# Weight sums of a Strassen-type product: four VectorE additions replaced by accumulating GpSimd transfers

## What is computed

```python
def swiglu(h, w_gate, w_up, w_down):
    return (jax.nn.silu(h @ w_gate) * (h @ w_up)) @ w_down

x = x + 0.5 * swiglu(rmsnorm(x, norm_ffn1), w1_gate, w1_up, w1_down)
...
x = x + 0.5 * swiglu(rmsnorm(x, norm_ffn2), w2_gate, w2_up, w2_down)
return rmsnorm(x, norm_final)
```

## Time and profile before

| | |
|---|---|
| runs | 2141.56, 1722.46, 1720.77 us; median 1722.46 |
| the profiled execution | 1721.32 us, of which 1719.5 us span |
| TensorE busy | 1706.5 us, 99% of the span |
| VectorE / ScalarE / GpSimd busy | 1226.1 / 845.6 / 204.8 us |
| granted TensorE clock | 0.999 over the span |
| moved | 346.28 MB, mean 201 GB/s |

### The profile page before, as it was taken

The page is one execution under the profiler, slowest core; times in us unless marked ns, Lnnn a source line. Parts: engine busy times, 40 slices in busy tenths (PEclk is TensorE's granted clock), DMA queues, the critical chain, the costliest instruction groups (busy, mean ns, idle before and its releaser), DMA issues.

```text
span 1719.5 us, 20848 instructions
## 1 busy us (share of the span) xinstructions
PE 1706.5 (99%) x7638; PEld 1414.8 (82%) x7638; DVE 1226.1 (71%) x1417; ACT 845.6 (49%) x989; POOL 204.8 (12%) x376
## 2 busy tenths in 40 slices
PE   9999999999999999999999999999999999999998
PEld 7788888888888888888888888888887888888886
DVE  7988888886555566587877888888888865554554
ACT  6555555554444444454554555555555554443443
POOL 0111111111110000000040001111111111100000
PEclk9999999999999999999999999999999999999999
DMA  8666666666665555665544565666666666655552
GB/s 293 190 215 216 213 214 217 213 209 209 207 208 196 196 195 191 209 202 192 170 153 164 196 196 179 216 214 214 213 217 197 216 220 203 232 190 193 193 195 98
DMA packets 186226, 346.28 MB, mean 201 GB/s; under 512 B 11768, under 2 KB 23984, under 8 KB 186032
## 3 DMA queue, kind: packets, MB, share of 16 engines
q1 hardware_dynamic: 172960, 332.51, 58.7%
q0 software_dynamic: 11264, 11.56, 2.4%
q10 hardware_dynamic: 1936, 1.32, 0.3%
HBM read 331.71 MB, written 2.10 MB: 194 GB/s over the span
## 4 chain that ended last, share of the span: by engine, by line
PE 96%; DVE 1%; issue 1%; ACT 1%; DMA 1%; POOL 0%; ACTq 0%; SPq 0%; DVEq 0%
PE banks L508 28%; PE banks L509 27%; PE banks L510 27%; PE banks L611 3%; PE banks L612 3%; PE banks L610 3%; PE banks L494 2%; PE banks L527 1%; PE banks L497 1%; POOL turned L1805 0%; DMA turned<-squared 0%; PE banks L704 0%; DVE w_lo L1412 0%; PE banks L728 0%; DVE w_lo L1181 0%
## 5 line engine op out<-in xcount | busy, mean ns | idle before, releaser
L1181 DVE TENSOR_TENSOR w_lo<-raw,w_hi 128x1024 fp32r<-128x1024 f32 x366 | 449.7, 1232 | 349.9 <-ACT w_hi L852 348.4
L852 ACT ACTIVATE w_hi<-raw 128x1024 fp32r<-128x1024 f32 x366 | 386.6, 1060 | 513.4 <-PE banks L510 487.6
L508 PE MATMUL banks<-w_hi,act 128*128 128x512 f32 x1280 | 499.1, 390 | 3.2 <-DVE w_lo L1412 3.2
L510 PE MATMUL banks<-w_lo,act 128*128 128x512 f32 x1280 | 498.0, 389 | 0.0
L509 PE MATMUL banks<-w_hi,act 128*128 128x512 f32 x1280 | 498.0, 389 | 0.0
L1412 DVE TENSOR_TENSOR w_lo<-raw,w_hi 128x1024 fp32r<-128x1024 f32 (+1 forms) x288 | 328.7, 1159 | 111.4 <-ACT w_hi L991 109.0
L991 ACT ACTIVATE w_hi<-raw 128x1024 fp32r<-128x1024 f32 (+1 forms) x288 | 286.9, 1010 | 223.7 <-PE banks L510 200.5
L508 PE MATMUL banks<-w_hi,h 128*128 128x512 f32 x832 | 323.8, 389 | 0.0
L510 PE MATMUL banks<-w_lo,h 128*128 128x512 f32 x832 | 323.7, 389 | 0.0
L509 PE MATMUL banks<-w_hi,h 128*128 128x512 f32 x832 | 323.7, 389 | 0.0
L508 PEld LDWEIGHTS banks<-w_hi,act 128*128 128x128 f32 x1280 | 240.3, 188 | 54.5 <-DVE w_lo L1412 4.4
(11 more groups left out here) (173 smaller groups left out, 1194.3 us busy)
## 6 DMA issues: line engine op xcount, KB each, us to landing
raw<-in_w_down SPq DMA_DIRECT2D x88, 1024.0 KB, 5.0
raw<-in_w_gate SPq DMA_DIRECT2D x84, 1024.0 KB, 5.3
raw<-in_w_up SPq DMA_DIRECT2D x84, 1024.0 KB, 5.5
raw<-in_w_in SPq DMA_DIRECT2D x32, 1024.0 KB, 5.2
raw<-in_w_out SPq DMA_DIRECT2D x16, 1024.0 KB, 5.0
turned<-squared POOLq DMA_DIRECT2D x320, 32.0 KB, 5.6
raw<-in_w_up SPq DMA_DIRECT2D x8, 512.0 KB, 9.2
raw<-in_w_gate SPq DMA_DIRECT2D x7, 512.0 KB, 9.5
```

The lines of the kernel that those rows point to most:

```text
L508: pe.matmul(dst, operand[:, k, hi], w_hi[:, s, w], start=k == first, stop=False)
L510: mm = pe.matmul(dst, operand[:, k, hi], w_lo[:, s, w], start=False, stop=k == last)
L852: act_e.activation(w_hi[:, s, :], raw[:, (p // 2) % RAW_SLOTS, off:off + PIECE], ACT.Copy).then_inc(hi_ready, 1)
L1181: dve.tensor_tensor(w_lo[:, s, :], raw[:, (p // 2) % RAW_SLOTS, off:off + PIECE], w_hi[:, s, :].bitcast(F32), ALU.subtract).then_inc(lo_re ...
```

## The change

The four sums leave VectorE. GpSimd begins four transfers per superblock that add into their destination (`accum_op=ALU.add`), each with a semaphore of its own, and the buffer `sums` goes:

- T3: low half of up chunk 0 += its high half (SBUF to SBUF), when the chunk has landed
- T1: low half of gate chunk 0 += the low half of up chunk 0, *read again from DRAM*, when piece 1 is split
- T2: the same place += the high half of up chunk 0 (SBUF to SBUF), when T1 (piece 7) is split
- T4: the same place += the high half of gate chunk 0 (SBUF to SBUF), when T2 (piece 11) is split, and behind the 16 transfers of `exchange` on GpSimd

The pieces change places: T3 is piece 5, T1 piece 7, B22 9, T2 11, T4 15. Since gate chunk 0's slot is now in use up to T4, chunks 6 and 7 change slots, chunk 7 may start only when 16 pieces are split, and with it everything that SP has behind it; chunk 2 may start only when the superblock before is wholly split. `square_h` goes from behind piece 11 to behind piece 6, `fold_gate` from behind 17 to behind 19.

```diff
-B11_0, B11_1, B21, T1, T3, B22, T2, T4 = 0, 1, 3, 5, 7, 9, 11, 13
+B11_0, B11_1, B21, T3, T1, B22, T2, T4 = 0, 1, 3, 5, 7, 9, 11, 15
-UP_AT = {14 + n: 4 + 2 * n for n in range(6)}
-SUMS = (T1, T3, T2, T4)
+UP_AT = {13: 4, 14: 6, 16: 8, 17: 10, 18: 12, 19: 14}
+SUMS = (T3, T1, T2, T4)
-FAST_SLOTS = (0, 1, 2, 3, 2, 3, 0, 1)
...
+FAST_SLOTS = (0, 1, 2, 3, 2, 3, 1, 0)
...
-FAST_FREE = (-6, -4, -2, 0, 5, 9, 12, 12)
+FAST_FREE = (-6, -4, 0, 0, 5, 9, 12, 16)
-FOLD_AT = (15, 16, 17)
-MERGE_AT, PRODUCT_AT, SQUARE_H_AT, SPLIT_FAST_AT = 2, 4, 11, 18
+FOLD_AT = (14, 16, 19)
+MERGE_AT, PRODUCT_AT, SQUARE_H_AT, SPLIT_FAST_AT = 2, 4, 6, 18
@@ SP, load_gate_up
+                    if i == FAST_SBS + 1 and c == 2:
+                        sp.wait_ge(lo_ready, first)
@@ ScalarE, round_fast
                 if p in SUMS:
-                    act_e.wait_ge(summed, 4 * nth + SUMS.index(p) + 1)
...
+                    act_e.wait_ge(summed[SUMS.index(p)], 16 * (nth + 1))
@@ VectorE: add_sum goes, with its four calls in fast_gate_up
-                    if p == B11_1:
-                        add_sum(nth, T1, turn, shift)
-                        add_sum(nth, T3, turn, shift)
-                    if p == B22:
-                        add_sum(nth, T2, turn, shift)
-                    if p == T2 - 1:
-                        add_sum(nth, T4, turn, shift)
@@ GpSimd
+            def add_weights(p, slot, src):
+
+                pool.dma_start(raw[:, slot, 0:PIECE].rearrange("p (t n) -> p t n", n=QCOLS), src,
+                               accum_op=ALU.add).then_inc(summed[SUMS.index(p)], 16)
+            def fast_sums(f, i):
+
+                first, shift = fast_first(f, i), 0 if i % 2 else 2
+                gate, up = FAST_SLOTS[0] + shift, FAST_SLOTS[1] + shift
+                pool.wait_ge(raw_landed[up], (f["turn"] + 2 * i + 1) * 16)
+                add_weights(T3, up, second_half(up))
+                pool.wait_ge(lo_ready, first + B11_1 + 1)
+                add_weights(T1, gate, f["up"][0:2 * P, i * QCOLS:(i + 1) * QCOLS]
+                            .rearrange("(t p) n -> p t n", p=P))
+                pool.wait_ge(lo_ready, first + T1 + 1)
+                add_weights(T2, gate, second_half(up))
+                exchange(f["sb"] + i - 1, turned)
+                pool.wait_ge(lo_ready, first + T2 + 1)
+                add_weights(T4, gate, second_half(gate))
```

More of the change, by code:

```diff
@@ L75 @@
 MID_FIRST = GATE_PIECES + ROW_PIECES
-B11_0, B11_1, B21, T1, T3, B22, T2, T4 = 0, 1, 3, 5, 7, 9, 11, 13
+B11_0, B11_1, B21, T3, T1, B22, T2, T4 = 0, 1, 3, 5, 7, 9, 11, 15
 GATE_AT = {2: 4, 4: 6, 6: 8, 8: 10, 10: 12, 12: 14}
-UP_AT = {14 + n: 4 + 2 * n for n in range(6)}
-SUMS = (T1, T3, T2, T4)
+UP_AT = {13: 4, 14: 6, 16: 8, 17: 10, 18: 12, 19: 14}
+SUMS = (T3, T1, T2, T4)
 S5, S7, S2, S12 = range(4)
 P1_BANK, N5_BANK, N7_BANK, R6_BANK = 4, 5, 6, 7
-FAST_SLOTS = (0, 1, 2, 3, 2, 3, 0, 1)
-FAST_CHUNK = {0: (0, 0), 1: (0, 1), 2: (2, 0), 3: (0, 2), 4: (2, 2), 6: (3, 0), 7: (1, 0), 8: (3, 2),
-              9: (1, 2), 10: (4, 0), 11: (1, 2), 12: (4, 2), 14: (5, 0), 15: (5, 2), 16: (6, 0),
-              17: (6, 2), 18: (7, 0), 19: (7, 2)}
-FAST_FREE = (-6, -4, -2, 0, 5, 9, 12, 12)
+FAST_SLOTS = (0, 1, 2, 3, 2, 3, 1, 0)
+FAST_CHUNK = {0: (0, 0), 1: (0, 1), 2: (2, 0), 3: (0, 2), 4: (2, 2), 5: (1, 0), 6: (3, 0), 7: (0, 0),
+              8: (3, 2), 9: (1, 2), 10: (4, 0), 11: (0, 0), 12: (4, 2), 13: (5, 0), 14: (5, 2),
+              15: (0, 0), 16: (6, 0), 17: (6, 2), 18: (7, 0), 19: (7, 2)}
+FAST_FREE = (-6, -4, 0, 0, 5, 9, 12, 16)
 COPY_P1_AT, ROUND_FAST_AT = 8, 17
-FOLD_AT = (15, 16, 17)
-MERGE_AT, PRODUCT_AT, SQUARE_H_AT, SPLIT_FAST_AT = 2, 4, 11, 18
+FOLD_AT = (14, 16, 19)
+MERGE_AT, PRODUCT_AT, SQUARE_H_AT, SPLIT_FAST_AT = 2, 4, 6, 18
 U0, W0 = 48, 64
@@ L189, in layer_kernel @@
         forms = at("forms", [P, 2, 4, 2, P], F32R, fast_at)
-        sums = at("sums", [P, PIECE], F32, fast_at + 8 * PIECE)
         whole = at("whole", [P, 4, 2, P], F32, fast_at + 8 * PIECE)
@@ L258, in layer_kernel @@
         h_squared = sem("h_squared")
-        summed = sem("summed")
+        summed = [sem(f"summed{p}") for p in SUMS]
         whole_act_ready = sem("whole_act_ready")
@@ L980, in round_fast @@
                 act_e.wait_ge(piece_used, first + p - SPLIT_SLOTS + 1)
+                c = FAST_CHUNK[p][0]
+                slot = (FAST_SLOTS[c] + shift) % RAW_SLOTS
                 if p in SUMS:
-                    act_e.wait_ge(summed, 4 * nth + SUMS.index(p) + 1)
-                if p in (T1, T4):
-                    dst, src = w_hi[:, p % SPLIT_SLOTS, :], sums[:, :]
-                else:
-                    c = FAST_CHUNK[p][0]
-                    slot = (FAST_SLOTS[c] + shift) % RAW_SLOTS
+                    act_e.wait_ge(summed[SUMS.index(p)], 16 * (nth + 1))
+                else:
                     act_e.wait_ge(raw_landed[slot], (turn + (1 if c < 4 else 2)) * 16)
-                    off, size = fast_part(p)
-                    dst, src = w_hi[:, p % SPLIT_SLOTS, 0:size], raw[:, slot, off:off + size]
-                act_e.activation(dst, src, ACT.Copy).then_inc(hi_ready, 1)
+                off, size = fast_part(p)
+                act_e.activation(w_hi[:, p % SPLIT_SLOTS, 0:size], raw[:, slot, off:off + size],
+                                 ACT.Copy).then_inc(hi_ready, 1)
             def copy_p1(first, fi):
@@ L1383, in split_forms @@
                 dve.memset(folds[:, :, :], 0.0).then_inc(folded, 1)
[L1385 to L1401, removed]
             def split_fast(first, p, shift):
@@ L1406, in split_fast @@
                 s = p % SPLIT_SLOTS
[L1407 to L1411, removed]
+                off, size = fast_part(p)
+                src = raw[:, (FAST_SLOTS[FAST_CHUNK[p][0]] + shift) % RAW_SLOTS, off:off + size]
                 dve.tensor_tensor(w_lo[:, s, 0:size], src, w_hi[:, s, 0:size].bitcast(F32),
@@ L1457, in fast_gate_up @@
             def fast_gate_up(f, i, shift):
-                turn, first, fi = f["turn"] + 2 * i, fast_first(f, i), f["sb"] + i
+                first, fi = fast_first(f, i), f["sb"] + i
                 nth = f["fast"] + i - 1
@@ L1806, in exchange, with second_half @@
                                      .rearrange("p (t k) j -> p t (k j)", k=SB)).then_inc(h_turned, 16)
+            def add_weights(p, slot, src):
+                pool.dma_start(raw[:, slot, 0:PIECE].rearrange("p (t n) -> p t n", n=QCOLS), src,
+                               accum_op=ALU.add).then_inc(summed[SUMS.index(p)], 16)
+            def second_half(slot):
+                return raw[:, slot, PIECE:2 * PIECE].rearrange("p (t n) -> p t n", n=QCOLS)
+            def fast_sums(f, i):
[11 more added lines that the diff above has]
+                add_weights(T4, gate, second_half(gate))
             for f in ffns:
-                for i in range(1, GATE_SBS):
+                for i in range(1, FAST_SBS + 1):
+                    fast_sums(f, i)
+                for i in range(FAST_SBS + 1, GATE_SBS):
                     exchange(f["sb"] + i - 1, turned)
```

## The result

The changed kernel takes 1805.09 us (1801.42 to 1808.14, four runs), the one before 1721.88 us beside it; the ratio is 1.0485, with an interval of 1.0465 to 1.0506. It is slower by 83 us. One run of before took 2141.56 us; the ratio is of the fast runs alone. The profiled execution took 1801.42 us, of which 1799.4 us are its span.

The account below looks back on a forecast made before the run. TensorE, busy 99% of the span, was taken to bound the kernel, hiding the removed VectorE additions (worth 0). The loop would lengthen superblocks from 42.2 to 47.4 us: 1721.3 + 15 x 5.2 = 1799.3, so 1800 us, range 1730 to 1890.

Parts of the forecast that it names:

- the loop paces: Fast superblocks: the feeding chain from T2 back to T2' sets the pace, X from 6.6 to 12; 1757 to 1920 us, chance 0.60.
- X: Time from issue to landing of one accumulating 512 KB GpSimd transfer: taken as 8.0 us, bounded by 3.3 and 14.1.
- 2X + 31.4: Superblock length in us if T4's issue waits for T2's landing, then round and split of piece 11.
- X + 38.0: Superblock length in us if the exchange on GpSimd, 8.9 us, holds T4's issue in place of T2's landing.
- step 6: After chunk 7 loads: round 18, split 18, split_h, split 19, together 4.6 us.
- T3 and T1 beside the loop: These two transfers lie outside the chain that sets a superblock's length; T1 has 13.9 us to spend.
- It closes 14 times, and half for the last ones: Seven closings per feed-forward part, each part's last superblock counted half: 15 x 5.2 = 78 us lost.
- The clock, for which I set no term: TensorE's clock: stalls of 1 to 4 us spread over 42 should not lower it from 2.4 GHz; no term.
- The signs I named: Exchanges 47 us apart, L1390 waits before pieces 2, 11 or 15 to 18, landing near 8 us, VectorE down 78 us.
- the bound of X = 14.1: Dearest transfer, with GpSimd's issue growing from 0.53 to 4.2 us: superblock 59.6 us, 17.4 us lost.
- Hidden: Rival: transfers land fast, X below 4.2, no TensorE wait at all; 1719 to 1722 us, chance 0.26.
- The DMA engines are the bound: Rival: addition slow inside DMA engines, X 12 and more, queued loads late too; 1900 to 2050 us, chance 0.13.

Follow-up runs that it names:

- experiment 4: Changed kernel with T2 alone made by VectorE, T3, T1 and T4 staying transfers: 1766.67 us, ratio 1.0255.
- experiment 2: Changed kernel with T2 and T4 made by VectorE, only T1 and T3 staying accumulating transfers: 1723.65 us, ratio 1.0007.
- experiment 5: Changed kernel with T1, T3 and T2 made by VectorE, only T4 staying an accumulating transfer: 1766.41 us, ratio 1.0258.
- experiment 1: Changed kernel, its piece order and load table kept, with all four sums made again by VectorE: 1725.88 us, ratio 1.0021.
- experiment 11: Kernel before the change with square_h behind piece 8 instead of 11, nothing else: 1719.50 us, ratio 0.9989.
- experiment 8: Changed kernel with all four transfers as plain copies, the sums left out: 1754.82 us, ratio 1.0199.
- experiment 6: Changed kernel with the exchange behind T4 on GpSimd instead of ahead of it: 1805.44 us, ratio 1.0485.
- experiment 7: Changed kernel with T2 made by VectorE and the exchange behind T4: 1771.62 us, ratio 1.0292.
- experiment 9: Changed kernel with T4's transfer alone a plain copy, its sum left out, the other three accumulating: 1784.20 us, ratio 1.0364.

## Why the prediction was right

The forecast was 1800 us, in a range of 1730 to 1890; measured are 1805. The case that came true is "the loop paces", with X between 6.6 and 12. Step by step, by the chain of after from 256.19, one of the four superblocks that close through chunk 2' as the forecast had it:

| step | forecast | measured |
|---|---|---|
| T2's issue to T4's issue, held by the exchange or by T2's landing | 8.9, or X + 2.3 = 10.3 | 9.1, held by the exchange; T2 lands in 6.1 |
| T4 lands | X = 8.0 | 7.4 |
| round and split 15 | 2.3 | 2.4 |
| chunk 7 | 5.3 | 5.1 |
| round 18 to split 19 | 4.6 | 4.9 |
| chunk 2' | 5.3 | 6.1 |
| round and split 2' | 2.3 | 2.4 |
| VectorE up to T2' | 9.3 | 9.6 |
| the superblock | 47.4 | 47.0 (this one), 47.5 (mean of 14) |

- **The size X** was mis-sized upward, and unequally. I took one X of 8.0 for both; T2 takes 6.2 and T4 7.4 on the mean. With T2 at 6.2 the branch 2X + 31.4 isn't the largest (6.2 + 2.3 = 8.5 < 9.1): the term that decides is X + 38.0, the one with the exchange, and by it the superblock would be 45.4.
- **The steps around it** made up for that: chunk 2' took 6.1 and not 5.3, VectorE and step 6 0.3 more each, the exchange 0.2 more. What isn't X measured 47.0 - 7.4 = 39.6 us where I had 38.0. That 47.4 met 47.5 is partly two errors of opposite sign, about 2.0 us down and 1.6 up per superblock. Experiment 4 says the same: T2's price comes mostly from its place in GpSimd's queue. Only once, at 1145.07, did T2 land late enough (8.6 us) to hold T4 itself, issued 11.3 us after it.
- **The way back to T2'** is a step that I had named only in part. I let the loop close through chunk 2'; in 8 of 14 links it closes through chunk 3' and piece 6', which the forecast doesn't have. Both ways are about equally long (47.0 and 47.2 us), so the sum didn't suffer: this too is luck.
- **T3 and T1 beside the loop**: held where it was tested. They took 9 to 10 us and cost nothing by themselves or beside T4 (experiments 2, 4 and 5), and TensorE didn't wait for pieces 5 and 7. The bound of 13.9 us for T1 was enough. Beside T2 and T4 together they share the time of chunk 3', and no run shows what that costs.
- **The order itself at 0**: it was 4 us, most of it one late split in every fast superblock (experiment 1), which I hadn't looked at.
- **"It closes 14 times, and half for the last ones"**: the 14 distances hold 74 us of the span's growth, the remaining 6 us lie outside them, where I had counted 5.2 for the two last superblocks.
- **The clock, for which I set no term**: wrong. See below. It cost nothing visible here.
- **The wait on the exchange in the kernel before**: right, experiment 11 takes away one of the two by starting it earlier.
- **The signs I named**: exchanges 47 us apart, waits at L1390, landing near 8 us and ScalarE waiting for `raw<-raw` all came. In the superblock from 256.19 TensorE waits before piece 15 (0.26 us), 18 (0.47) and 2' (2.58), as named, but also before piece 0' (0.95), which I hadn't: ScalarE rounds it behind `silu_fast`, and that waits for `fold_gate` (70.6 us over the 16 superblocks). VectorE fell by 71 us, not 78. The issue stayed at 0.9 to 1.3 us, so the bound of X = 14.1, where it would grow to 4.2, was far off.

On the rivals. *Hidden* needed X under 4.2. As plain copies the transfers come near that, T2 at 3.0 and T4 at 4.7, and the kernel still took 32 us more than before (experiment 8), since the rest of the loop is longer than I had it: 39.6 + 4.7 = 44.3, and 44.4 were measured. *The DMA engines are the bound* fell: T1 and T3 are free by themselves and beside T4, and one transfer alone, T4, costs 40.5 us. Yet the engines aren't without part in it. Here are the windows of one superblock of after (busy us and instructions of PE, PEld, DVE, ACT, POOL, then clock, DMA share, GB/s):

```profile
256.20:303.20 47.00, 42.75 (x185) 34.17 (x184) 30.61 (x32) 21.85 (x24) 12.53 (x21) 1.00 0.83 234
```

The share is 0.83 over a longer superblock, where it was 0.64; loads of gate chunks take 6.1 instead of 5.3 us at the median. That is the size of the 0.8 us of chunk 2' in the table.

**The two pages.** T2 takes 6.2 us as an accumulating transfer and 3.0 us as a copy (experiment 8). "DMA: Bandwidth & Descriptors", section "Anatomy of one DMA — SWDGE (gpsimd) path", in the Trainium skill gives 3.2 us for 512 KB. The copy in T2's place agrees with it (3.0; what moved in these 3.0 us, at 196 GB/s, was little more than its own bytes), the transfers that this kernel makes don't, with 7.4 at the median. The engines' own time says where at least a part of it comes from. Queue q0 took 13.0% of 1799.4 us, less 2.4% of 1719.5 for the exchange, which is 193 us or 3.0 us for each of 64 transfers; as copies it is (7.5% of 1752.1 - 41.3) / 64 = 1.4 us. That is twice, as the Trainium skill has it in "Collectives: The Full Stack", section "The bandwidth ceiling: the fold count and why AG ≠ RS ≠ AR", where it speaks of transfers between cores: an added block needs two source reads. So the trace agrees with that rule for the engines' time; the 8.8 us by it was nearer to T4's 7.4 than the 3.2 was.

**What stays open.** Why T4 lands 1.2 us later when it is issued 0.7 us earlier, ahead of the exchange (experiments 6 and 7), and why a copy in T4's place takes 6.5 us among accumulating transfers and 4.7 among copies (experiment 9). Contention with the chunk loads that begin at the same split is likely, but no run separates it. And beside T4, T2 costs 38 us by the medians (experiment 4 against after), where 15 x 1.7 = 26 are explained by the queue. The two profiled executions differ by only 1799.4 - 1772.0 = 27 us, near what is explained; that kernel's four runs spread over 9 us (1764.71 to 1773.77), and why is open. So is what T3 and T1 cost through chunk 3' when all four sums are transfers.

## What to carry to other kernels

A sum of 1.2 us on an engine with room to spare became a transfer of 6 to 10 us that keeps a slot in use. Ask of each such move not how much the engine saves, but whether the landing stands in a loop that closes from one stage to the next (transfer, piece, freed slot, load, piece), and add that loop up around: two of the four transfers here were free at 9 to 10 us, and one at about 7 us cost 40 us. When the loop has parallel branches, work out which is longest with each one's own duration; shortening another, as in experiment 6, brings nothing.

## What the runs showed of the hardware that I hadn't expected

- **Four accumulating transfers of 512 KB land 2 to 3 us later than four copies, each in its place**: T2 6.2 against 3.0 us, T4 7.4 against 4.7, T3 9.7 against 7.7 (without the program's first, which lands in 4.7 and 3.4), T1 (from DRAM) 8.9 against 6.0. With T4 alone a copy, only 0.9 us of its 2.7 is gained (experiment 9). GpSimd's issue grows too, from 0.55 to 0.87 us and more (0.72 to 1.20 for the DRAM one).
- **A short fall of TensorE's clock.** In after there are six stretches of 3.4 us in which the granted clock is 0.5, the 1.2 GHz level (from 199.9, 387.7, 1135.2, 1326.3, 1374.1, 1421.9 us). Before has none until its end. The first of them, in the windows of after and in TensorE's timeline ahead of it:

```profile
199.90:203.30 3.40, 3.40 (x9) 2.66 (x8) 3.40 (x5) 1.06 (x1) 0.00 (x0) 0.51 1.10 266
193.00:200.00 7.00, 3.55 (x15) 2.31 (x14) 3.44 (x4) 4.67 (x7) 1.20 (x1) 1.00 1.02 284
```

```profile
194.97 0.50 PE L611 MATMUL banks<-w_hi,act 128*128 128x512 f32 x1 [0.95 <-DVE w_lo L1390]
...
199.13 0.50 PE L509 MATMUL banks<-w_hi,act 128*128 128x512 f32 x1 [2.49 <-DVE w_lo L1390]
...
200.34 0.63 PE L510 MATMUL banks<-w_hi,act 128*128 128x512 f32 x1
```

In the 7 us ahead of it TensorE was busy for 3.55 us and waited for 0.95 and 2.49; then matmuls take 0.63 and not 0.40 us. Each dip costs 1.7 us of work at full clock. It isn't seen in the time: from exchange to exchange the superblocks with a dip took 46.9 to 48.7 us (mean 47.4), those without 46.6 to 49.4 (mean 47.5), because TensorE isn't what paces them. Were it the pacer, six dips would be 10 us. The kernel of experiment 1, which TensorE does pace, has one such dip, from 59.4 us, behind its wait of 3.38 us. So my sentence that such stalls should not lower the clock was wrong, and a forecast for a kernel that TensorE paces would have missed a term.
